# Block one's projections z, v and g: from direct products to Strassen's seven

## What is computed

```python
h = layer_norm(x, ln_emb_g, ln_emb_b)
proj = jnp.einsum("bsd,de->bse", h, w_in)
z, xbc, dt_f, dt_b, q, k, v, g = jnp.split(proj, offs, axis=-1)
...
zg = jax.nn.silu(z)                      # gates the state space branch
o = diff_attention(q, k, v, lam, slopes)
o = rms_norm(o, subln_g) * (1.0 - lam_init)
y_attn = o * jax.nn.silu(g)              # gates the attention branch
```

## Time and profile before

| | |
|---|---|
| median of 3 runs | 3054.57 us (3054.49 to 3057.16) |
| the profiled execution | 3058.05 us, its span 3056.2 us |
| PE busy | 2892.2 us, 95% of the span |
| PE weight loads | 2294.2 us, 75% |
| DVE busy | 2172.2 us, 71% |
| ACT busy | 1253.4 us, 41% |
| POOL busy | 695.7 us, 23% |
| z, v and g projections | from about 17 us to 297.4 us |

### The profile page before, as it was taken

The page is one execution under the profiler, slowest core; times in us unless marked ns, Lnnn a source line. Parts: engine busy times, 40 slices in busy tenths (PEclk is TensorE's granted clock), DMA queues, the critical chain, the costliest instruction groups (busy, mean ns, idle before and its releaser), DMA issues. The chain is left out here.

```text
span 3056.2 us, 39152 instructions
## 1 busy us (share of the span) xinstructions
PE 2892.2 (95%) x14592; PEld 2294.2 (75%) x14592; DVE 2172.2 (71%) x3406; ACT 1253.4 (41%) x2296; POOL 695.7 (23%) x572
## 2 busy tenths in 40 slices
...
GB/s 254 127 99 63 98 73 142 183 148 130 211 80 84 125 59 214 163 91 76 42 111 228 158 140 179 98 96 59 28 17 81 86 137 98 111 222 123 110 110 56
DMA packets 214824, 359.77 MB, mean 118 GB/s; under 512 B 16675, under 2 KB 118211, under 8 KB 214635
## 3 DMA queue, kind: packets, MB, share of 16 engines
...
## 5 line engine op out<-in xcount | busy, mean ns | idle before, releaser
L4283 PE MATMUL banks<-b3down_r_t 128*128 128x512 f32 x1344 | 308.2, 392 | 12.2 <-DVE b3down_r_t L4315 11.4
L4283 PEld LDWEIGHTS banks<-b3down_r_t 128*128 128x128 f32 x1344 | 254.2, 189 | 66.2 <-DVE b3down_r_t L4315 11.8
L431 PE MATMUL banks<-b1ln_w,b_hThi 128*128 128x512 f32 x768 | 239.5, 393 | 3.2 <-DVE b_hTlo L338 3.2
L533 PE MATMUL banks<-b_hThi,b1item_hi 128*128 128x512 f32 x464 | 195.0, 420 | 3.4 <-DVE b1item_lo L522 3.1
L4040 PE MATMUL banks<-b3up_t_t,b3up_w_w 128*128 128x512 f32 x768 | 184.2, 396 | 3.1 <-DVE b3up_w_w L3997 3.1
L2358 PE MATMUL banks<-b2h_hi,b2h_whi 128*128 128x512 f32 (+1 forms) x448 | 178.4, 398 | 4.8 <-DVE b2h_lo L1764 2.4
L533 PE MATMUL banks<-b_hThi,b1item_lo 128*128 128x512 f32 x464 | 181.5, 391 | 0.0
L533 PE MATMUL banks<-b_hTlo,b1item_hi 128*128 128x512 f32 x464 | 180.9, 390 | 0.0
L2358 PE MATMUL banks<-b2h_lo,b2h_whi 128*128 128x512 f32 (+1 forms) x448 | 177.0, 395 | 0.0
L2358 PE MATMUL banks<-b2h_hi,b2h_wlo 128*128 128x512 f32 (+1 forms) x448 | 176.7, 394 | 0.0
L4040 PEld LDWEIGHTS banks<-b3up_t_t,b3up_w_w 128*128 128x128 f32 x768 | 145.3, 189 | 37.7 <-DVE b3up_w_w L3997 3.5
...
## 6 DMA issues: line engine op xcount, KB each, us to landing
...
b1out_ws<-in_w_out SPq DMA_DIRECT2D x16, 1024.0 KB, 5.1
b3upr_raw<-in_w_mlp_up SPq DMA_DIRECT2D x16, 1024.0 KB, 5.0
b3down_a_t<-act_spill SPq DMA_DIRECT2D x16, 1024.0 KB, 4.9
b3down_b_t<-in_w_mlp_down SPq DMA_DIRECT2D x16, 1024.0 KB, 7.4
...
act_spill<-b3upc_c POOLq DMA_DIRECT2D x13, 1024.0 KB, 4.6
```

The costliest lines, as they stand in the source:

```text
L431: last = pe.matmul(K.bank[n % 6], a, b, start=part + k + c == 0, stop=part + k + c == 6)
L533: last = K.pe.matmul(pair[:, ss], a, b, start=q % 2 == 0 and i == 0, stop=q % 2 == 1 and i == 11)
L4283: last = pe.matmul(K.bank[b], x[:, q, cols], y[:, q], start=c == 0, stop=c == 11)
```

## The change

The three projections are each done as a product of 2 x 2 blocks of 512 x 512, by the form of Strassen's method that has seven block products instead of eight and fifteen block sums. With h = (h11, h12; h21, h22) and a weight B: product 1 is h11 B11, 2 is h12 B21, 3 is s4 B22, 4 is h22 times a sum of B, 5 is s1, 6 is s2 and 7 is s3 times sums of B, where s1 = h21 + h22, s2 = s1 - h11, s3 = h11 - h21, s4 = h12 - s2. `SEVEN` is the order of the 21 products. A product is four row tiles x 4 contraction tiles x 3 passes = 48 matmuls into four banks (`nat_banks`); its weights come as two units of [128, 2, 512].

- **Weights.** Five slots of a unit's two parts. A unit's raw data is loaded into the slot itself, once the unit four before it has been used (`unit_done`; for products 3 and 4 of the list, counted from 0, the whole product must be over). Units of kinds 5 and 7 take two loads of 512 KB, the others one. POOL does the subtraction of blocks for kinds 5, 7, 6 and 4 (`pool_unit`, 1024 elements a partition), then ACT (`unit_hi`) and DVE (`unit_lo`) split.
- **Input sums.** ACT copies the turned tile a second time (`row`: 1024 elements for the first four row tiles, 512 for the last four), DVE adds two instructions of 512 elements to `turned_lo` of the last four; `sum_hi` and `sum_lo` split the four sums; DVE makes s2 and POOL s4 by one instruction of 2048 elements each.
- **During the norm.** Rows 0 to 3 take products z 1 and z 2 (24 matmuls a row tile, as before), then come v 1 and v 2, which need only the first half of the sequence, then z 5.
- **Results.** One instruction takes four banks (2048 elements): ACT copies kinds 1, 5 and 7, DVE adds kinds 2, 6, 4 and 3 to tiles in SBUF and does three more additions after kind 6 (`combined`). Silu runs on ACT from SBUF to SBUF. Stores are of 1024 KB.
- **The other table.** `pe_rows` and `act_rows` stand after the last product, `sp_rows` after product g 6, `sp_rows_out` in `sp_conv` behind the first two items' loads, ahead of `norm_over`. `item(1)` waits for `rows_out`.

Semaphores later shared by other stages are renumbered; the rest of the program is the same.

```diff
-NAT = [("z", 0), ("z", 1), ("v", 0), ("v", 1), ("g", 0), ("g", 1)]
-NAT0 = {"z": Z0, "v": V0, "g": G0}
-NAT_N = len(NAT) * ST
+ZVG0 = {"z": Z0, "v": V0, "g": G0}
+SEVEN = [("z", 1), ("z", 2), ("v", 1), ("v", 2)] + [(w, i) for w in "zv" for i in (5, 7, 6, 4, 3)] + [("g", i) for i in (1, 2, 5, 7, 6, 4, 3)]
+SEVEN_AT = {x: n for n, x in enumerate(SEVEN)}
+NAT_MM = 8 + 2 * (len(SEVEN) - 2)
...
+def unit_done(u):
+
+    n = u // 2
+    if n < 2:
+        return 7 + n
+    return 8 + 2 * (n - 2) + (2 if n in (3, 4) else u % 2 + 1)
+
+
+def product_done(n):
+    return 8 + 2 * (n - 1)
...
+def unit_slot(K, u):
+
+    return K.p1.slot[u if u <= 4 else (u + 3) % 4]
...
+def sp_unit(K, u):
+
+    sp, S, L = K.sp, K.S, K.loads
+    (w, i), part = SEVEN[u // 2], u % 2
+    if u >= 5:
+        sp.wait_ge(S["nat_mm"], unit_done(u - 5 if u < 9 else u - 4))
+    block = lambda k, n: K.w1[k * 512 + part * 256:k * 512 + part * 256 + 256, ZVG0[w] + n * 512:ZVG0[w] + (n + 1) * 512].rearrange("(k p) n -> p k n", p=P)
+    raw_hi, raw_lo = unit_raw(K, u)
+    if i == 5:
+        if w == "z":
+            sp.wait_ge(S["nat_mm"], unit_done(4))
+        else:
+            sp.wait_ge(S["nw_lo"], 2 * SEVEN_AT[("z" if w == "v" else "v", 4)] + part + 1)
+        L.start(sp, ("nat_t", u), K.p1.t[part], block(0, 1))
+        L.start(sp, ("nat_hi", u), raw_hi, block(0, 0))
+    elif i == 7:
+        L.start(sp, ("nat_lo", u), raw_lo, block(0, 1))
+        L.start(sp, ("nat_hi", u), raw_hi, block(1, 1))
+    elif i in (6, 4):
+        L.start(sp, ("nat_hi", u), raw_hi, block(1, 1) if i == 6 else block(1, 0))
+    else:
+        L.start(sp, ("nat_lo", u), raw_lo, {1: block(0, 0), 2: block(1, 0), 3: block(1, 1)}[i])
...
+def pool_unit(K, u):
+
+    g, S, L = K.g, K.S, K.loads
+    (w, i), part = SEVEN[u // 2], u % 2
+    if i not in (5, 7, 6, 4):
+        return
+    t, (raw_hi, raw_lo) = K.p1.t[part], unit_raw(K, u)
+    g.wait_ge(*L[("nat_hi", u)])
+    if i == 5:
+        g.wait_ge(*L[("nat_t", u)])
+        last = g.tensor_tensor(t, t, raw_hi, ALU.subtract)
+    elif i == 7:
+        g.wait_ge(*L[("nat_lo", u)])
+        last = g.tensor_tensor(raw_lo, raw_hi, raw_lo, ALU.subtract)
+    else:
+        g.wait_ge(S["nw_lo"], 2 * SEVEN_AT[(w, 5 if i == 6 else 6)] + part + 1)
+        last = g.tensor_tensor(t, raw_hi, t, ALU.subtract)
+    last.then_inc(S["nat_t"], 1)
+
+
+def unit_hi(K, u):
...
+    w, i = SEVEN[u // 2]
+    if i in (1, 2, 3):
+        a.wait_ge(*K.loads[("nat_lo", u)])
+    else:
+        a.wait_ge(S["nat_t"], NAT_T.index((w, i, u % 2)) + 1)
+    a.activation(unit_slot(K, u)[0], unit_source(K, u), ACT.Copy).then_inc(S["nw_hi"], 1)
...
     def turned_lo(st):
+
         v.wait_ge(S["ln_hi"], st + 1)
         cols = slice(st * P, (st + 1) * P)
-        v.tensor_tensor(K.hTlo[:, :, cols], by_k(K.pair[3]), K.hThi[:, :, cols], ALU.subtract).then_inc(S["ln_lo"], 1)
-
-    def gated(n):
-
-        v.wait_ge(S["nat_act"], n + 1)
-        if n == 4 * ST:
-            v.wait_ge(*K.loads["subln"])
-            K.vs.mark(v.tensor_scalar(m.sub, m.sub, 1.0 - LAM_INIT, None, ALU.mult))
-            v.wait_ge(K.vs.sem, K.vs.n)
-        tile = m.out[n % 4].rearrange("p (h e) -> p h e", h=4)
-        v.tensor_tensor(tile, tile, over(m.sub, 1, 4), ALU.mult).then_inc(S["nat_g"], 1)
+        turned = by_k(K.pair[3])
+        last = v.tensor_tensor(K.hTlo[:, :, cols], turned, K.hThi[:, :, cols], ALU.subtract)
+        if st >= 4:
+            cols = slice((st - 4) * P, (st - 3) * P)
+            s1, s2, s3 = m.s1[:, :, cols], m.s2[:, :, cols], m.s34[:, 0:4, cols]
+            K.vs.mark(v.tensor_tensor(s3, s3, turned[:, 0:4], ALU.subtract))
+            last = v.tensor_tensor(s1, s2, turned[:, 0:4], ALU.add)
+        last.then_inc(S["ln_lo"], 1)
...
+    def first(r):
+
+        v.wait_ge(S["nat_act"], copied_at("z", 1, r))
+        v.wait_ge(S["nat_mm"], 2 * r + 2)
+        v.tensor_tensor(m.out[1][:, r], m.out[0][:, r], K.bank[(2 * r + 1) % 6], ALU.add).then_inc(S["nat_sum"], 1)
...
+    def combined(n):
+
+        w, i = SEVEN[n]
+        if i != 6:
+            return
+        u, c, d = (nat_tile(K, w, end) for end in ("c12", "c22", "c21"))
+        v.wait_ge(S["nat_sum"], summed_at(w, "u1"))
+        v.wait_ge(S["nat_act"], copied_at(w, 7))
+        then(v.tensor_tensor(d, d, u, ALU.add))
+        K.vs.mark(v.tensor_tensor(u, u, c, ALU.add))
+        v.tensor_tensor(c, c, d, ALU.add).then_inc(S["nat_sum"], 1)
+        v.wait_ge(K.vs.sem, K.vs.n)
...
     front(0)
     normed(0)
-    split_lo(K, 0)
+    unit_lo(K, 0)
     turned_lo(0)
-    split_lo(K, 1)
+    unit_lo(K, 1)
+    unit_lo(K, 2)
+    unit_lo(K, 3)
     front(1)
     for st in range(1, ST):
         normed(st)
+        if 2 <= st < 6:
+            first(st - 2)
+        for u in {3: (4,), 5: (5,), 6: (6, 7)}.get(st, ()):
+            unit_lo(K, u)
         if st + 1 < ST:
             front(st + 1)
         turned_lo(st)
-    split_lo(K, 2)
-    split_lo(K, 3)
-    for n in range(ST, NAT_N):
-        w, st = n // ST, n % ST
-        if st in (2, 4) and w + 1 < len(NAT) and 2 * (w + 1) + (st == 4) >= 4:
-            split_lo(K, 2 * (w + 1) + (st == 4))
-        if NAT[w][0] == "g" and n >= 4 * ST:
-            gated(n)
+        if st == ST - 2:
+            sum_lo(0)
+    unit_lo(K, 8)
+    unit_lo(K, 9)
+    sum_lo(1)
+    v.wait_ge(K.vs.sem, K.vs.n)
+    v.tensor_tensor(m.s2, m.s2, m.s34[:, 0:4], ALU.subtract).then_inc(S["h7_sum"], 1)
+    for n in range(4, len(SEVEN) + 1):
+        evacuated(n - 1)
+        if n == 4:
+            sum_lo(2)
+        unit_lo(K, 2 * n + 2)
+        combined(n - 1)
+        unit_lo(K, 2 * n + 3)
+        if n in (5, 6):
+            sum_lo(n - 2)
+        if n >= 5:
+            gated(n - 2)
+    gated(len(SEVEN) - 1)
...
+def sum_pieces(K):
+
+    m = K.p1
+    return [(m.s1hi, m.s1lo, m.s1, slice(0, 384)), (m.s1hi, m.s1lo, m.s1, slice(384, 512)), (m.s3hi, m.s3lo, m.s34[:, 0:4], slice(0, 512)), (m.s2hi, m.s2lo, m.s2, slice(0, 512)), (m.s4hi, m.s4lo, m.s34[:, 4:8], slice(0, 512))]
...
+    def row(st):
+        a.wait_ge(S["ln_turned"], st + 1)
+        turned, cols = by_k(K.pair[3]), slice(st % 4 * P, st % 4 * P + P)
+        a.activation(K.hThi[:, :, st * P:(st + 1) * P], turned, ACT.Copy)
+        if st < 4:
+            last = a.activation(m.s34[:, :, cols], turned, ACT.Copy)
+        else:
+            last = a.activation(m.s2[:, :, cols], turned[:, 4:8], ACT.Copy)
+        last.then_inc(S["ln_hi"], 1)
...
+    unit_hi(K, 0)
     for st in range(ST):
-        a.wait_ge(S["ln_turned"], st + 1)
-        a.activation(K.hThi[:, :, st * P:(st + 1) * P], by_k(K.pair[3]), ACT.Copy).then_inc(S["ln_hi"], 1)
+        row(st)
         if st == 0:
-            split_hi(K, 1)
-        if st in (4, 5):
-            split_hi(K, st - 2)
-        if st:
-            evacuated(st - 1)
-    for n in range(ST - 1, NAT_N):
-        w, st = n // ST, n % ST
-        if n >= ST and st in (2, 4) and w + 1 < len(NAT) and 2 * (w + 1) + (st == 4) >= 4:
-            split_hi(K, 2 * (w + 1) + (st == 4))
-        evacuated(n)
-        if ST < n <= ST + ROW_PIECES:
-            act_rows(K, n - ST - 1)
+            for u in (1, 2, 3):
+                unit_hi(K, u)
+        if 1 <= st < 5:
+            first(st - 1)
+        for u in {2: (4,), 4: (5,), 5: (6, 7), 6: (8,)}.get(st, ()):
+            unit_hi(K, u)
+        if st == ST - 2:
+            sum_hi(0)
+            evacuated(2)
+            unit_hi(K, 9)
+            silu(1)
+    sum_hi(1)
+    sum_hi(2)
+    for n in range(4, len(SEVEN) + 1):
+        if n > 4:
+            evacuated(n - 1)
+        unit_hi(K, 2 * n + 2)
+        unit_hi(K, 2 * n + 3)
+        if n in (5, 6):
+            sum_hi(n - 2)
+        if n == len(SEVEN):
+            for i in range(ROW_PIECES):
+                act_rows(K, i)
+        if n > 4:
+            silu(n - 1)
...
     turn(0)
-    for n in range(ST):
-        job(n, 0)
-        if n + 1 < ST:
-            turn(n + 1)
-        job(n, 1)
-    for n in range(ST, NAT_N):
+    for r in range(4):
+        if r == 0:
+            pe.wait_ge(S["nw_lo"], 1)
+        pe.wait_ge(S["ln_lo"], r + 1)
+        if r == 3:
+            pe.wait_ge(S["nat_act"], copied_at("z", 1, 0))
+        matmuls(0, r, 0, K.bank[2 * r % 6])
+        turn(r + 1)
+        if r == 0:
+            pe.wait_ge(S["nw_lo"], 2)
+        matmuls(0, r, 1, K.bank[2 * r % 6]).then_inc(S["nat_mm"], 1)
+        if r == 0:
+            pe.wait_ge(S["nw_lo"], 4)
+        elif r == 3:
+            pe.wait_ge(S["nat_sum"], summed_at("z", "c11", 0))
         for part in range(2):
-            job(n, part)
-        if ST < n <= ST + ROW_PIECES:
-            pe_rows(K, n - ST - 1)
+            last = matmuls(1, r, part, K.bank[(2 * r + 1) % 6])
+        last.then_inc(S["nat_mm"], 1)
+    pe.wait_ge(S["nat_act"], copied_at("z", 1, 2))
+    pe.wait_ge(S["nat_sum"], summed_at("z", "c11", 2))
+    for part in range(2):
```

(53 more changed lines are left out.)

278 lines of the change are left out of this document (190 added, 88 removed), and 4 rows, old and new, of the table TAKEN_OVER.

## The result

The changed kernel takes 3084.97 us (median of 4 runs, 3082.88 to 3085.95), the kernel before 3055.86 us (4 runs, 3054.49 to 3057.47). The ratio is 1.0094, with a 95% interval of 1.0079 to 1.0108: 29 us slower. I had forecast 3054, and at most 3067. The profiled execution has a span of 3081.1 us, 24.9 more than that of before.

What follows compares the result with a forecast made beforehand. PE was taken to bound the kernel, with DVE not far below until 83.4 us. 32.6 us removed less 22.5, 4.9 and 4.4 left 0.8 off the 3054.57 median: 3054 us, range 3041 to 3067.

Steps and rivals of the forecast that it cites:

- Removed: Projections: six jobs of 48, 144 matmuls at 226.7 ns, 32.6 us, all on PE's path.
- Place one: The norm, first five products: PE gaps of 3.7, 5.1 and 4.0 us, clock losses and POOL's 1.2; 22.5 us lost.
- the banks' 5.1: After two of v 2's row tiles PE waits for ACT's copy of v 1's banks: idle 5.1 us.
- the walk: The step-by-step chain of times through the norm and products, ending the fifth product at 105.9 us.
- My rule by the length of a gap: After PE gaps: the lowered clock costs 0 to 1.6 us; 1.6 taken for all of 3.6 us and more.
- Place two: Before product z 6: units 12 and 13 load late, idle 3.3 us and 1.6 of clock, 4.9 (bounds 2.5 and 7.4).
- The slower rival: From z 4 on: POOL delays splits by 1.5 us in each of nine products, giving 3067 us; chance 0.25.
- the faster one: Places one and two: no clock losses, no POOL 1.2, place two 2.5; gain 10.8, 3044 us; chance 0.30.
- Place three: From the last projection matmul to item(0): 13.8 us and 1.6 of clock against 11.0 before; 4.4 us lost.
- The sum of places one to three: Whole change: 32.6 - 22.5 - 4.9 - 4.4 = 0.8 us gained.
- The rows' way through DRAM and the last store are hidden.: After the projections: item 2's lo part ready about 30 us after the last product, PE asks at 37; no cost.
- the third rival: Item 2: last store beside the spreading makes it 3 us late, 4.6 with clock, 3058.5 us; within the forecast's 0.45.

Runs made afterwards that it cites:

- experiment 6: The changed kernel with the spreading on 16 engines, plus the split of s2 ahead of the splits of z 6's weights on ACT and DVE: 3053.85 us.
- Experiment 2: The changed kernel with only the spreading's dimensions reordered, the 128 copies slowest in place of the 4 rows: 3059.06 us, ratio 1.001.
- experiment 8: The changed kernel with 16-engine spreading, plus splits of items 0 and 1 ahead of the last evacuations and table pieces behind item(0): 3066.32 us.
- experiment 1: The changed kernel with the spreading of the two tables issued behind the loads of items 2 and 3: 3077.11 us, ratio 1.007.
- experiment 3: The kernel before, without Strassen's products, with only sp_rows_out moved behind the last projection product: 3079.53 us, ratio 1.0076.
- experiment 11: The changed kernel with the norm's instructions reordered and s2's split ahead of z 6's splits, the spreading unchanged: 3066.94 us, ratio 1.0041.

## Why the prediction was wrong

The steps, in its order:

1. **Removed: 32.6 us.** Right. 144 matmuls fewer, and z 7, from z 5's end at 108.65 to 119.69 us, takes 11.0.
2. **Place one, 22.5 us lost.** Right in mechanism. All three gaps are where they were walked: v 2's 3.7 is 5.53, the banks' 5.1 is 4.58, z 5's 4.0 is 3.67. v 2's is longer because POOL's 2.76 us stretched two splits to 4.50, of which I had taken 1.2 us. The three together are 13.8 us, for 14.0 with POOL's 1.2. z 5 starts at 95.01; the walk has 93.4 (89.4 and 4.0). The clock cost more than its bound behind each gap, where I had given 0 to 1.6: v 2's first row tile takes 4.4 us from 69.91 and its third 4.8 from 82.72 in place of 2.72, and z 5 13.6 in place of 10.88, so 1.7, 2.1 and 2.8 us are lost. The five products end at 108.65, not 105.9. My rule by the length of a gap was not borne out even by my own rows: the earlier trace rows has a gap of 2.49 us ahead of eight transposes that take 1.94 us in place of 1.04, at clock 0.50, and I set only the 2.88 and 3.63 against the 3.06 that kept its clock. On POOL and DVE the rule that the prediction cites from the Trainium skill, GPSIMD Engine Reference, section 1, Specifications, contention where a DVE instruction has two SBUF inputs, agrees with the trace: 8.97 us for two splits beside POOL's 7.95 and 4.77. But it is not always DVE that is held, as I had read it: POOL's second subtraction, from 99.87, took 4.46 us in place of 2.4, while DVE's split of s3, begun at 99.78 with both inputs in SBUF, kept its 2.29.
3. **Place two, 4.9.** The gap before z 6 is 4.65 for 3.3, with POOL in DVE's way once (3.77 us at 120.47 for a split of 2.29 elsewhere), which the bound had. The trace names ACT's `b1ln_out` for this gap, but s2's split ends at 124.24, just ahead of PE's 124.34, and experiment 6 moves nothing but that split's place. From z 7's end at 119.69 to the last product's end, 289.37, are 15 products of 10.88 and 6.5 us more; so place two costs 6.5, within its bounds of 2.5 and 7.4.
4. **No wait after it.** Right: from z 6 to the table pieces PE has no wait, and is busy for 50.00 of 50 us. The slower rival, POOL holding up the splits product after product, didn't happen, and neither did the faster one: in the changed kernel every one of the five gaps is followed by the lower clock.
5. **Place three, 4.4.** 12.3 us from 289.37 to `item(0)` for 13.8, so a little too dear. `item(0)` is 0.8 us later than before, plus the clock behind its gap.
6. **The sum of places one to three.** Forecast 0.8 us gained. Experiment 2, where nothing else costs, has its span 1.6 us over the span of before, and a ratio of 1.001. So the sum is off by 2.4 us by the spans and 4.8 by the medians. By `item(0)` it is 3.0: the walk has it at 298.7 (105.9 + 10.88 + 4.9 + 15 x 10.88 + 13.8), the trace at 301.64, with places one and two 4.5 us dearer than forecast and place three 1.5 cheaper. That the error is so small is in part luck, since these have opposite signs.
7. **"The rows' way through DRAM and the last store are hidden."** This is the step that failed, with the 7 us of margin of the third rival that rests on it. It is a term put at nothing. I moved a step and priced its wait for PE, but not its transfer: the prediction names the spreading's 3.8 MB beside a store of 1024 KB and gives them no duration, and the 30 us to item 2's lo part have no working. The transfer takes 43 us, from its issue at 299 us to where SP's wait for it ends, about 342, and moves 105 to 107 GB/s from 311.5 us on. At the 407 GB/s that experiment 2 has for 5 us it would take 9 to 10, an estimate; there the spreading and the last store are both over 16 us after the first issue (299.06 to 315.22). PE asked for item 2 as forecast, 36 us after the last product (325.4; I had 37), but the item was ready at 59.6 in place of 30 (289.37 to 348.94): not 3 us late but 23.5. The trace of before had the sign: at 115 us the issue of `toe_wide` lasts 7.10 us, and from 120 to 142 us the DMA engines go at a share of 0.35 and 138 GB/s, other traffic included. I made nothing of the first and didn't read the second, since under the projections the transfer costs nothing.

Why 105 GB/s: the edit of experiment 2 changes the order of the dimensions and no byte, and the rate goes up fourfold. The share of 0.26 to 0.28 of 16 engines is that of four of them at work, and 4 is the number of rows, the slowest dimension before the edit; with 128 the share is 1.03. By these shares an engine moves about 26 GB/s before the edit and 25 after it (105 by 4, 407 by 16), so that the number of engines accounts for the difference. The profile shows only their mean; that it was four is read from it. This agrees with the Trainium skill, DMA: Bandwidth & Descriptors, under "Why a DMA increments its semaphore by 16 and not by 1": the number of engines of a transfer is the largest up to 16 that divides the slowest dimension of both sides. That the later loads are held in their issue (16.31, 18.24, 18.10 and 16.53 us in the changed kernel and experiments 1, 3 and 11) is measured. That it ends with the 16-engine form is shown by experiment 8 and not by 2, where the transfer was over when the 8 KB load was issued: in 8 that load was issued at 311.79, 1.1 us behind `toe_wide`, and took 0.37. Which resource runs full is not shown. How much of the rest is the queue and how much the reuse of a lane (5.1 us of wait) no run separates cleanly: experiment 1, which takes the lane's wait off the items, keeps three quarters of the loss.
